# Two expert pairs gathered at once into transposed form, and three instructions moved elsewhere

## The reference

```python
for layer in range(2):
    x = x + mixer(rms_norm(x, ln_mix))            # attention + DeltaNet, or retention
    h = rms_norm(x, ln_ffn[layer])
    group = top1(softmax(h @ w_rg + b_rg))        # 4 groups of 8 experts
    experts, p = top2(softmax((h @ w_re + b_re)[group]))
    for each token's two experts e, with gate = p_group * p_e / sum(p):
        hid = silu(h @ w_gate[e]) * (h @ w_up[e])   # 1024 -> 512
        x += gate * (hid @ w_down[e])               # 512 -> 1024
```

## Time and profile before

| | us |
|---|---|
| median of 3 runs | 1784.76 |
| profiled execution: its own time | 1781.61 |
| its span | 1779.7 |
| PE busy | 1738.8 |
| weight loads on PE (overlapping) | 1110.3 |
| DVE busy | 659.1 |
| ACT busy | 444.4 |
| POOL busy | 211.9 |
| gate and up matmuls (L1682, 2048) | 448.3 |
| gather matmuls (L1653, 512) | 138.9 |

### The profile page before, as it was taken

The page is one execution under the profiler, slowest core; times in us unless marked ns, Lnnn a source line. Parts: engine busy times, 40 slices in busy tenths (PEclk is TensorE's granted clock), DMA queues, the critical chain, the costliest instruction groups (busy, mean ns, idle before and its releaser), DMA issues.

```text
span 1779.7 us, 23446 instructions
## 1 busy us (share of the span) xinstructions
PE 1738.8 (98%) x9329; PEld 1110.3 (62%) x9329; DVE 659.1 (37%) x1158; ACT 444.4 (25%) x864; POOL 211.9 (12%) x152
## 2 busy tenths in 40 slices
PE   7999999999999999999999999999999999999998
PEld 6778988654544445454888888887654544445453
DVE  3775774423232323234413223132523232323233
ACT  4465643211111111112332323313311111111110
POOL 2400100100000000001534343432000000000000
PEclk9999999999999999999999999999999999999999
DMA  8410112599999999998122122122499999999996
GB/s 195 99 48 1 49 50 95 213 390 409 409 409 410 410 410 410 410 409 327 48 89 81 68 95 95 64 96 78 189 369 409 409 410 410 409 410 410 409 410 239
DMA packets 141177, 460.39 MB, mean 259 GB/s; under 512 B 5552, under 2 KB 31376, under 8 KB 140208
## 3 DMA queue, kind: packets, MB, share of 16 engines
q1 hardware_dynamic: 140368, 457.01, 66.1%
q0 software_dynamic: 736, 2.34, 1.1%
HBM read 457.24 MB, written 2.10 MB: 258 GB/s over the span
## 4 chain that ended last, share of the span: by engine, by line
PE 49%; DVE 1%; issue 0%; ACT 0%; DVEq 0%
PE bank L153 20%; PE bank L1682 12%; PE bank L1693 6%; PE bank L1700 3%; PE bank L1653 3%; PE bank L2201 1%; PE bank L1658 1%; PE bank L2255 0%; PE bank L1687 0%; PE bank L1481 0%; PE bank L1667 0%; PE bank L1469 0%; DVE X L1981 0%; DVE X L1976 0%; PE bank L1562 0%
## 5 line engine op out<-in xcount | busy, mean ns | idle before, releaser
L1682 PE MATMUL bank<-ring,SCR 128*64 128x512 f32 x2048 | 448.3, 593 | 1.1 <-DVE SCR L1662 0.9
L153 PE MATMUL bank<-ring_r 128*128 128x512 f32 (+2 forms) x1216 | 360.5, 379 | 6.8 <-DVE ring_r L399 2.5
L1682 PEld LDWEIGHTS bank<-ring,SCR 128*64 128x64 f32 x2048 | 152.0, 137 | 291.0 <-issue 284.2
L153 PEld LDWEIGHTS bank<-ring_r 128*128 128x128 f32 x1216 | 225.9, 192 | 49.6 <-issue 3.6
L2132 POOL TENSOR_TENSOR ring_r<-ring,ring_r 128x1024 fp32r<-128x1024 f32 x62 | 150.7, 2465 | 709.6 <-DVE ring_r L2132 482.1
L1693 PE MATMUL bank<-ring,SCR 128*64 128x512 f32 x1024 | 226.8, 595 | 0.0
L1976 DVE TENSOR_TENSOR X<-X,bank 128x512 f32<-128x512 f32 x240 | 153.8, 682 | 96.5 <-PE bank L1700 96.4
L1712 DVE SCALAR_TENSOR_TENSOR SCR<-SCR,bank 128x512 f32<-128x512 f32 x32 | 23.9, 748 | 359.7 <-PE bank L1682 359.7
L1700 PE MATMUL bank<-SCR_r 128*128 128x512 f32 x512 | 152.8, 419 | 1.6 <-DVE SCR_r L1709 0.8
L1693 PEld LDWEIGHTS bank<-ring,SCR 128*64 128x64 f32 x1024 | 70.7, 137 | 132.3 <-issue 128.6
L153 PE MATMUL bank<-ring_r,SCR_r 128*128 128x512 f32 x576 | 140.3, 399 | 2.0 <-DVE X L2386 2.0
(11 more groups left out here) (404 smaller groups left out, 1711.2 us busy)
## 6 DMA issues: line engine op xcount, KB each, us to landing
ring<-in_w_gate_dram SPq DMA_DIRECT2D x64, 2048.0 KB, 15.1
ring<-in_w_up_dram SPq DMA_DIRECT2D x64, 2048.0 KB, 18.4
ring<-in_w_down_dram SPq DMA_DIRECT2D x64, 2048.0 KB, 14.8
ring<-in_w_in_odd_dram SPq DMA_DIRECT2D x8, 2048.0 KB, 8.9
ring<-in_w_in_even_dram SPq DMA_DIRECT2D x16, 512.0 KB, 6.8
ring<-in_w_in_odd_dram SPq DMA_DIRECT2D x8, 1024.0 KB, 8.2
ring<-in_w_out_odd_dram SPq DMA_DIRECT2D x4, 2048.0 KB, 7.7
ring<-in_w_out_even_dram SPq DMA_DIRECT2D x2, 2048.0 KB, 8.3
```

Source lines behind the costliest of these rows:

```text
L153: mm = pe.matmul(out, lhs[a], rhs[b], start=(first and i == 0), stop=(last and i == 2))
L1682: mm = pe.matmul(bank[SLOTS * u:SLOTS * u + SLOTS, :], x_tile(k, u), w[u][:, k, :], start=(k == 0), stop=(k == KT - 1))
```

## The change

- Two pairs are gathered at once, in odd pairs: the one-hots of pairs i+1 and i+2 stand side by side (`OH2`, 256 columns). The tokens are the stationary operand and OH2 the moving one, so the product comes out transposed (features by slots) and goes, times the gain, straight to the operand of gate and up (`XT2`). 64 matmuls of 256 columns in four groups of 16 replace, for two pairs, 32 of 512 columns, 16 transposes, 4 copies on ACT; DVE's copies stay four for two pairs.
- Groups 0 and 1 wait for the bank as before; group 2 waits for copy 0, group 3 for copy 1 (banks 0 and 1 in turn). Before the loop four other banks are used, so there are no such waits.
- PE's and DVE's order in even pairs is without gathers, and the two halves of down stand between combines. DVE makes both one-hots at the end of the even pair.
- Attention: the wait for the gate stages goes behind projection 0, which uses bank 3 instead of 7; the convolution weights' transpose waits for the first four copies only.
- Retention, head 0: VL[0] between the two rotations, the second of which uses other scratch memory. Last head: the lower part of tile 3 behind the first add.

```diff
-            pe.wait_ge(*g_stage("g_gates"))
+            pe.wait_ge(sg("a_proj_out"), 4)
             pe.wait_ge(params_in, PARAMS)
             pe.wait_ge(consts_in, 16)
             pe.transpose(PB[2][:, 0:48], cwr[0:48, :], ident[0:48, 0:48]).then_inc(sg("d_cw"), 1)
+            gproj_pe(pe, 0)
+            pe.wait_ge(*g_stage("g_gates"))
...
-            for n in range(5):
+            for n in range(1, 5):
                 gproj_pe(pe, n)
             pe.wait_ge(sg("d_conv_ready"), 1)
+            g_left_bank(pe, 0)
...
-            return PB[(7, 5, 4, 7, 5)[n] if n < 5 else (7, 5, 7)[(n - 5) % 3]]
+            return PB[(3, 5, 4, 7, 5)[n] if n < 5 else (7, 5, 7)[(n - 5) % 3]]
...
+        def pairs_mm(pe, bank, q, lower_ready=None):
+            for j in range(2):
+                k = 2 * q + j
+                at = slice((k % 2) * 512 + k // 2, (k % 2 + 1) * 512, 4)
+                for i, part in enumerate((XNU, XN_r)):
+                    for t in range(NT):
+                        if i and not t and not j and lower_ready:
+                            pe.wait_ge(*lower_ready)
+                        mm = pe.matmul(bank[:, j * 256:(j + 1) * 256], part[:, t, at], OH2[:, t, :], start=(t + i == 0), stop=(t == NT - 1 and i == 1))
+            return mm
+
+        def pairs_copy(dve, l, bank, q):
+            return dve.tensor_tensor(XT2[:, 2 * q:2 * q + 2, :], bank[:, :].rearrange("p (k n) -> p k n", k=2),
+                                     gcol[:, l, 2 * q:2 * q + 2, None].to_broadcast([P, 2, 2 * P]), ALU.mult)
...
             def pair(i, b):                      # experts_pe
-                gate(i)
-                up(i)
+                gate(i, b)                       # waits for the copies only if b == 0
+                up(i, b)
...
+                if is_at(i, 0):
+                    hidden_t(i)
+                    slots_transposed(i + 1)
+                    down(i, (0, 1))
+                elif b == 0:
+                    combine(i - 1, 1 - b, (0, 1))
+                    hidden_t(i)
+                    combine(i - 1, 1 - b, (2, 3))
+                    slots_transposed(i + 1)
+                    down(i, (0,))
+                    combine(i - 1, 1 - b, (4, 5))
+                    down(i, (1,))
+                    combine(i - 1, 1 - b, (6, 7))
+                elif more:
+                    combine(i - 1, 1 - b, (0, 1))
+                    gather(i + 1, 0)
+                    hidden_t(i)
+                    combine(i - 1, 1 - b, (2, 3))
+                    gather(i + 1, 1)
+                    combine(i - 1, 1 - b, (4, 5))
+                    gather(i + 1, 2)
+                    combine(i - 1, 1 - b, (6, 7))
+                    slots_transposed(i + 1)
+                    gather(i + 1, 3)
+                    down(i, (0, 1))
...
-                if more:                         # experts_act, pair
-                    x_gathered(i + 1, 0)
...
                 hidden(i, b)                     # experts_dve, pair
+                if b and more:
+                    adds(i - 1, (0, 1))
+                    x_out(i + 1, 0)
+                    adds(i - 1, (2, 3))
+                    x_out(i + 1, 1)
+                    adds(i - 1, (4, 5))
+                    x_out(i + 1, 2)
+                    adds(i - 1, (6, 7))
+                    x_out(i + 1, 3)
+                else:
+                    adds(i - 1, range(8))
+                if b == 0 and not is_at(i, last - 1):
+                    dve.wait_ge(*mw("gat", 2 * i + 4))
+                    dve.wait_ge(*mw("ohg", i + 2))
+                    for u in range(2):
+                        one_hots(i + 2 + u, u).then_inc(ms("oh"), 1)
                 y_out(i)
 
-            one_hots(0).then_inc(ms("oh"), 1)
+            one_hots(0, 0).then_inc(ms("oh"), 1)
+            one_hots(1, 1).then_inc(ms("oh"), 1)
             lower_dve(dve, l, NT - 1)
             gates_dve(dve, l, step)
...
-            rotate(0, both)                      # ret_dve
+            rotate(0, both[0:1])
+            v_lower(0, 0)
+            rotate(0, both[1:2], [OY[:, t, :] for t in range(NT)])
...
-                for t in range(2) if h < RH - 1 else range(1, NT):
+                for t in range(2) if h < RH - 1 else range(1, 3):
                     yt_lower(h, t)
...
                     if h == RH - 1:
+                        if n == 0:
+                            yt_lower(h, 3)
```

More of the change, by code:

```diff
@@ L1646, in one, with first_bank, gather_mm @@
             return slice(e, e + 1) if isinstance(e, int) else bass.ds(e, 1)
-        def gather_mm(pe, half, lower_ready=None):
+        def first_bank(q):
+            return (PB[0], PB[1], PB[2], PB[4])[q]
+        def pairs_mm(pe, bank, q, lower_ready=None):
[11 more added lines that the diff above has]
+                                     gcol[:, l, 2 * q:2 * q + 2, None].to_broadcast([P, 2, 2 * P]), ALU.mult)
+        def gather_mm(pe, half):
             for i, part in enumerate((XNU, XN_r)):
                 for t in range(NT):
-                    if i and not t and lower_ready:
-                        pe.wait_ge(*lower_ready)
-                    mm = pe.matmul(BX[half][:, :], OH[:, t, :], part[:, t, half * 512:(half + 1) * 512], start=(t + i == 0), stop=(t == NT - 1 and i == 1))
+                    mm = pe.matmul(BX[half][:, :], OH_OF[0][:, t, :], part[:, t, half * 512:(half + 1) * 512], start=(t + i == 0), stop=(t == NT - 1 and i == 1))
             return mm
@@ L1674, in ot_ones, with x_tile, hidden_mm @@
             return dve.tensor_scalar(OT[b], OTG[b], 0.0, None, ALU.is_gt)
-        def x_tile(k, u):
-            return XTt[:, k, u * SLOTS:(u + 1) * SLOTS]
-        def hidden_mm(pe, bank, us, w):
+        def x_tile(k, u, b):
+            return XTt[:, k, u * SLOTS:(u + 1) * SLOTS] if b is None else XT2[:, k, b * P + u * SLOTS:b * P + (u + 1) * SLOTS]
+        def hidden_mm(pe, bank, us, w, b=None):
             for k in range(KT):
                 for u in us:
-                    mm = pe.matmul(bank[SLOTS * u:SLOTS * u + SLOTS, :], x_tile(k, u), w[u][:, k, :], start=(k == 0), stop=(k == KT - 1))
+                    mm = pe.matmul(bank[SLOTS * u:SLOTS * u + SLOTS, :], x_tile(k, u, b), w[u][:, k, :], start=(k == 0), stop=(k == KT - 1))
             return mm
@@ L1761, in hidden_t, with down @@
                 ht_mm(pe).then_inc(ms("ht"), 1)
-            def down(i):
+            def down(i, halves):
                 for u in range(2):
@@ L1768, in down @@
                 pe.wait_ge(*mw("ht_out", i + 1))
-                for half in range(2):
+                for half in halves:
                     down_mm(pe, half, range(2), w_two(l, 4, 4)).then_inc(ms("y"), 1)
@@ L1779, in combine, with gather @@
                     comb_mm(pe, comb_bank(m), m, b).then_inc(ms("comb"), 1)
[L1781 to L1784, removed]
-                        pe.wait_ge(*mw("xn_upper", NT))
[L1786 to L1792, removed]
+            def gather(i, q):
+                first = is_at(i, 0)
+                if q == 0:
+                    pe.wait_ge(*mw("oh", i + 2))
+                    if first:
+                        pe.wait_ge(*mw("xn_upper", NT))
+                if not first:
+                    pe.wait_ge(*(mw(("sil", "hh")[q], i) if q < 2 else mw("xt_out", 2 * i + q - 1)))
+                pairs_mm(pe, first_bank(q) if first else BX[q % 2], q, mw("xn_lower", NT) if first and q == 0 else None).then_inc(ms("gat"), 1)
             def slots_transposed(i):
@@ L2012, in experts_dve @@
             dve.wait_ge(*mw("oh", 1))
-            gated(0).then_inc(ms("ohg"), 1)
-            x_out(0, 0)
-            x_out(0, 1)
+            gated(0, 0).then_inc(ms("ohg"), 1)
+            for q in range(4):
+                x_out(0, q)
             pairs_loop(dve, pair)
```

89 lines of the change are left out of this document (35 added, 54 removed).

## The result

The kernel after takes 1886.32 us (median of 4 runs, 1884.94 to 1891.17), the kernel before 1784.51 beside it (4 runs, 1782.05 to 1790.21). The ratio is 1.058, 95% interval 1.055 to 1.060: 102 us slower. Forecast were 1801 and a range of 1780 to 1814. The direction was right, the size was not, and 94 of the 102 us go when one thing is changed, the distance between the columns of a stationary tile.

What follows compares the result with a forecast made beforehand. Weight transfers pace the expert stages, PE the rest. Terms + 7.0 + 5.0 + 11 + 1.7 - 4.3 - 3.9 = + 16.5 us take the profiled 1781.61 to 1798.1; with 3.15 to the runs' median, 1801 us, range 1780 to 1814.

Steps and rivals of the forecast that it cites:

- What bounds the kernel: Expert stages: transfers at 409 to 410 GB/s set the pace, 455.07 us from gate(0)'s release to the last gate's end.
- The price of a gather matmul: Expert loop, odd pairs: 0.12 us per 256-column matmul, 7.68 us for 64; bounds 0.10 and 0.23.
- the queue's start: Expert stages: 4.51 us for starting a load queue that has run dry and for the landing.
- the bound of the odd pair: Expert loop: upper bound of 1.4 us standstill per odd pair, if the new waits add a microsecond.
- the new waits: Odd pairs: gather 2 waits for copy 0, gather 3 for copy 1; might add a microsecond.
- Rival (2): Expert loop: odd pair longer than 26.57 us, by waits or slower stride-4 loads; another microsecond makes 14 us; chance 0.08.
- Rival (1): Expert loop: the clock stays up, 1790 us, no measurable change; chance 0.27.
- The dry queue: Expert loop: odd pairs release down slots 0.36 us too late, 7 times per layer; + 5.0 us for both layers.
- Before the loop: Gathers ahead of each expert loop: gate(0) 3.5 us later per layer, + 7.0 us in all; bounds + 4 and + 9.
- The clock in the loop: PE's 2.6 us gap before each odd pair's up lowers the clock in 6 of 14, 1.87 us each: + 11 us.
- Attention: Attention stage: PE waits some 5.8 us before projection 4 and loses the clock; + 1.7 us, bounds - 6.1 and + 3.2.
- Retention: Retention layer: first head's v stall and last head's residual-add stall go, with their clock losses; - 4.3 and - 3.9 us.

Runs made afterwards that it cites:

- the mended kernel: Kernel after, tokens stored so each feature tile is every second column, residual read in adjacent pairs: 1790.3 us (ratio 1.005); without the attention edit 1788.2 (1.004).
- the kernel with one tile at stride 4: Kernel after with one of eight feature tiles loaded from every fourth column, seven from every second (feature order not the reference's): 1794.8 us, one run.
- the kernel with two tiles at stride 4: Kernel after with two of eight feature tiles loaded from every fourth column, the others from every second (feature order not the reference's): 1816.4 us, one run.

## Why the prediction was wrong, step by step

**What bounds the kernel: right.** The expert stage is paced by the loads, the freed matmuls, copies and transposes bought next to nothing (an expert stage of 454.0 instead of 455.07 in the mended kernel), and unevenness between pairs turned into a dry queue, 7 times per layer.

**The price of a gather matmul: the step that failed.** I took 0.12 us, "the nearest form", from the earlier trace rows, where the stationary columns are at stride 2. The change's are at stride 4, and there it is 0.227. I had the second number in the text, as the upper bound of 0.23 (from another form), and did not carry it: 64 x 0.11 = 7 us per odd pair, 14 times, is 98 us, and the range should have reached to 1900. (With 0.227 in all its places and no loss of clock the sum gives some 1900; most of the 14 us down to the measured 1886 is the queue's start, near 3.5 us here and not 4.51, 14 times.) Instead the bound of the odd pair, 1.4 us, came from "the new waits" alone. Rival (2) named "a slower load of stride-4 columns", priced at one microsecond, with a chance of 0.08. It was that rival, seven times as large. Rival (1), the clock stays up and 1790, is near what the kernel with its load mended measured (1790.3), though that time has other parts: more before the loops, less in the retention.

**The dry queue: right in kind.** 6.2 us per two pairs instead of 0.36. With the load mended, the odd pair takes 26.6 us, as forecast, and two pairs 61.4, and no standing still remains. So 0.36 was already too much: the kernel with one tile at stride 4 held 61.4 us with an odd pair of 27.45, its next up 3.3 us behind the six chunks and not 4.51.

**Before the loop.** Forecast + 3.5 per layer, measured + 10.4 and + 11.2. The gather to gate(0)'s start is 16.42 us in layer 1 (1329.29 to 1345.71), where I had 9.45; the difference of 6.97 is 64 x 0.109. The other 0.7 lie ahead of the first gather, which came 15.44 us behind the first up issue (1313.85), where I had 14.8. With adjacent columns it is 10.35 in layer 0, of which 1.27 is a wait for the slower last lower tile.

**The clock in the loop: wrong, by its premise.** The gap before each odd up is 1.3 us in the mended kernels and not 2.6: the even pair's work, cut in two down halves among the combines, is longer by some 0.8 us than I had, and two pairs shorter by 0.36. In 142 such gaps, all that the traces of the nine kernels with the experts' edit show, the 32 matmuls behind took 7.09 us, except in four: there they took 8.78, after gaps of 1.98, 2.11, 2.18 and 2.36 us. 14 other gaps of 1.95 to 3.09 us cost nothing, nor did any shorter one. One that did, in the kernel with two tiles at stride 4, and the stretch behind it (the clock is the 0.81):

```profile
647.13 8.78 PE L1703 MATMUL bank<-ring,SCR 128*64 128x512 f32 x32 [2.36 <-DMA ring<-in_w_up_dram]
```

```profile
647.00:656.00 9.00, 8.87 (x33) 3.31 (x34) 0.00 (x0) 0.00 (x0) 0.00 (x0) 0.81 1.03 410
```

So + 11 us should have been near 0 (in the kernel after no gap of the loop cost anything); the 1.87 per loss was about right (1.69).

**Attention: right.** The answer to the earlier trace rows:

```profile
77.63 0.79 PE L153 MATMUL bank<-ring_r 128*128 128x512 f32 x1 [5.25 <-DVE ring_r L421]
...
85.67 0.60 PE L466 MATMUL bank<-CE,SCR 128*128 128x128 f32 x4
```

The wait moved to projection 4, the clock fell behind it, and it ends at 85.67 (forecast 85.65, before 83.94). In this execution the 1.7 us were made up by 100 us, since the kernel before ran at a granted clock of 0.83 from 90 to 100 us and this one at 1.00; alone the edit measured + 1.6, with an interval that reaches to 0.

**Retention: right, and partly hidden.** The answers to the earlier trace rows from 1284.87 on, and ahead of them the start of the first head's v:

```profile
924.44 1.05 PE L2208 MATMUL bank<-XN,CE 128*128 128x128 f32 x8
...
1284.87 5.74 PE L153 MATMUL bank<-ring_r,SCR_r 128*128 128x512 f32 x24
1290.45 0.63 PE L2280 MATMUL bank<-CE,SCR 128*128 128x128 f32 x4
1290.84 5.73 PE L153 MATMUL bank<-ring_r,SCR_r 128*128 128x512 f32 x24
1296.40 1.04 PE L1474 MATMUL bank<-CE,X 128*128 128x128 f32 x8
1297.20 3.00 PE L153 MATMUL bank<-ring_r,SCR_r 128*128 128x512 f32 x12
```

From 924.44 to 1284.87 it is 360.43 us against 364.69 before (867.31 to 1232.00): - 4.26, forecast - 4.3. From 1284.87 to 1297.20 it is 12.33 against 16.21 (to 1248.21): - 3.88, forecast - 3.9. But the stage as a whole gained only 4.7, because its opening lost 3.45, which I had nowhere: 1.07 us for the last up's load to arrive, and some 2.4 through PE's wait ahead of the first transposes:

```profile
895.30 3.61 PE L340 MATMUL bank<-CE,X 128*128 128x128 f32 x16 [2.87 <-DVEq L2049]
```

PE reached them 2.87 us earlier, at the same distance from the last combines as before, when it went straight on; the adds on DVE ran on the same schedule. Behind the wait the granted clock was 0.58 and 0.57 from 895 to 899 us, and the 16 transposes took 3.61 us (2.01 in the mended kernel); against that, PE's next wait was 0.38 us instead of 2.02. The wait is there in all nine kernels with the experts' edit (1.9 to 2.9 us) and in none of the four without. What in that edit causes it stays open.

## What to carry to other kernels

Before giving an operand a strided slice, look at the stride in bytes (only 4-byte elements were measured here): a row of the trace at stride 2 does not price the same instruction at stride 4. When the path is set by loads whose slots an engine frees, moving that engine's work from one iteration to the next is not free even if the sum falls: compare the longest stretch between two releases with the loads' period. And a bound once written down has to be multiplied through to the range.

## What the runs showed of the hardware

A 128x128 stationary load of 4-byte elements took 193, 197, 330 and 338 ns at a column stride of 1, 2, 4 and 8; where these loads follow each other one by one under 256-column matmuls, the load sets the pace at 0.23 us. ACT and DVE slowed too: 1024 elements in 1230 and 1278 ns at stride 2, 2257 and 2178 at stride 8, and DVE read adjacent pairs 32 bytes apart at full rate (256 elements in 481 ns). Strides between 2 and 8 were not tried on them. A standstill of PE of 1.95 to 3.09 us between full-size matmuls brought the clock down in four cases of 18, 1.69 us each time, with no length that separates them. A stream of 2 MB loads that had run dry took 3.2 to 5.8 us beyond the time of its six chunks until the matmuls that waited for it went on.
